# Fused hybrid layer: merge transfers issued by ScalarE, a full-width sine product on VectorE, and score blocks in another order

## What is computed

```python
qa, ka, va, ... = split(rmsnorm(x) @ w_in)          # 12 query heads, 4 key/value heads of 128
qa = apply_rope(rmsnorm(qa), cos, sin) * 128**-0.5  # rope: [t1*cos - t2*sin, t2*cos + t1*sin]
ka = apply_rope(rmsnorm(ka), cos, sin)
# three query groups with (window, dilation) = (128,1), (512,4), (2048,16):
#   causal dilated softmax attention over blocks of 128 queries, previous + own block of keys
o, lse = dilated_group(q[:, :, g], k, v, window, dilation)   # for g in 0, 1, 2
w = softmax(stack(lses)); oa = sum(w * outs)                 # the "merge" of the three groups
```

## Time and profile before

| what | value |
|---|---|
| median of three runs | 1892.96 us |
| profiled execution, its own time | 1892.71 us |
| its span, first to last instruction | 1891.2 us |
| TensorE busy / VectorE / ScalarE / GpSimd | 95% / 58% / 37% / 29% |
| heads 0 to 3 of mixer A (to the transposition of their statistics) | end at 198.5, 333.2, 465.4, 598.2 us |

### The profile page before, as it was taken

One profiled execution on the slowest core, in us unless ns is written; L12 is line 12 of the kernel. 1 busy time (PEld: TensorE's weight loads), 2 busy tenths in 40 slices (PEclk: granted clock), 3 DMA queues, 4 the chain that ended last, 5 costly groups with the idle time before them and its releaser, 6 DMA issues. The chain is left out here.

```text
span 1891.2 us, 27575 instructions
## 1 busy us (share of the span) xinstructions
PE 1797.0 (95%) x9188; PEld 1521.5 (80%) x9188; DVE 1101.1 (58%) x1928; ACT 700.6 (37%) x1598; POOL 551.1 (29%) x654
## 2 busy tenths in 40 slices
PE   6999989999989899999997999999999999999999
PEld 6888877878877888888895888877888888888887
DVE  5362462562652966667576554587555555566786
ACT  5233233233243335353536222453333333334443
POOL 2020230320412705151412000006565555620120
PEclk9999999999999899999999999999999999999999
DMA  7311321421221211111015323214232323178764
GB/s 201 100 35 50 91 95 34 116 74 61 79 78 46 68 46 46 35 33 55 28 72 197 120 83 112 101 67 134 94 105 100 116 89 111 70 251 318 257 213 171
DMA packets 169173, 196.42 MB, mean 104 GB/s; under 512 B 9488, under 2 KB 119344, under 8 KB 168576
## 3 DMA queue, kind: packets, MB, share of 16 engines
q1 hardware_dynamic: 154832, 156.59, 25.9%
q0 software_dynamic: 7984, 28.29, 4.5%
q10 hardware_dynamic: 6272, 10.49, 1.5%
HBM read 150.88 MB, written 44.45 MB: 103 GB/s over the span
## 5 line engine op out<-in xcount | busy, mean ns | idle before, releaser
L2228 PE MATMUL bank<-act_hi,w_hi 128*128 128x512 f32 x568 | 229.1, 403 | 3.9 <-DVE act_lo L1862 3.6
L2230 PE MATMUL bank<-act_hi,w_lo 128*128 128x512 f32 x568 | 222.8, 392 | 0.0
L2229 PE MATMUL bank<-act_lo,w_hi 128*128 128x512 f32 x568 | 222.2, 391 | 0.0
L2228 PE MATMUL bank<-ca,wq 128*128 128x512 f32 x528 | 206.9, 392 | 6.7 <-DVE wq L1973 4.3
L2230 PE MATMUL bank<-ca,wq 128*128 128x512 f32 x528 | 206.0, 390 | 0.0
L2229 PE MATMUL bank<-ca,wq 128*128 128x512 f32 x528 | 205.9, 390 | 0.0
L2228 PE MATMUL bank<-w_hi,act_hi 128*128 128x256 f32 (+1 forms) x576 | 181.3, 315 | 4.0 <-DVE act_lo L1543 3.1
L2229 PE MATMUL bank<-w_lo,act_hi 128*128 128x256 f32 (+1 forms) x576 | 177.7, 308 | 0.0
L2230 PE MATMUL bank<-w_hi,act_lo 128*128 128x256 f32 (+1 forms) x576 | 177.6, 308 | 0.0
L2228 PEld LDWEIGHTS bank<-act_hi,w_hi 128*128 128x128 f32 x568 | 107.6, 189 | 27.6 <-DVE act_lo L1862 4.8
L2230 PEld LDWEIGHTS bank<-act_hi,w_lo 128*128 128x128 f32 x568 | 107.2, 189 | 23.2
(11 more groups left out here) (364 smaller groups left out, 4295.1 us busy)
## 6 DMA issues: line engine op xcount, KB each, us to landing
w_raw<-in_w_in SPq DMA_DIRECT2D x60, 512.0 KB, 4.0
rawd<-in_w_ffn_down SPq DMA_DIRECT2D x99, 256.0 KB, 5.0
rx<-y_scratch SPq DMA_DIRECT2D x77, 256.0 KB, 4.3
wr<-in_w_ffn_gate SPq DMA_DIRECT2D x11, 1024.0 KB, 5.5
wr<-in_w_ffn_up SPq DMA_DIRECT2D x11, 1024.0 KB, 5.4
y_scratch<-sq SPq DMA_DIRECT2D x11, 1024.0 KB, 4.3
y_scratch<-yq SPq DMA_DIRECT2D x33, 256.0 KB, 2.1
gate_scratch<-gbuf ACTq DMA_DIRECT2D x32, 256.0 KB, 2.1
```

What stands on the lines that cost most here:

```text
L2228: pe.matmul(ps, lhs_hi, rhs_hi, start=first, stop=False, skip_group_check=onto)
L2229: pe.matmul(ps, lhs_hi, rhs_lo, start=False, stop=False, skip_group_check=onto)
L2230: return pe.matmul(ps, lhs_lo, rhs_hi, start=False, stop=last, skip_group_check=onto)
```

## The change

Three things are changed, all in mixer A.

1. The merge's transfers are issued by ScalarE and no longer by GpSimd. The store of the statistics stands at the end of `act_head_a`; the eight loads after the squares of s = 0 of the next head; the weights' store at the end of s = 4 and their broadcast load at the end of s = 5. For head 3 they stand at s = 0, 2 and 3 of mixer B's first head.
2. The sine product is one VectorE operation on all 512 columns; GpSimd's half of it is gone (`pool_rope` becomes `pool_rstd`), and so are the waits on `t1_sin`. The subtraction and the addition read the other halves.
3. The order of the batches and their places change. `UNITS` lists the pairs of blocks; the first batch stands at s = 3, two steps stand at s = 8, 11, 13 and 14 (before: 10 to 14). On VectorE `merge_norm` moves from behind `rope(3)` to inside `qk_norm(3)`, and `merge_mul` from s = 5, 8, 8 to s = 6, 7, 8.

```diff
+    def store_stats(eng, h):
+        eng.wait_ge(stat_sbd, h + 1)
+        eng.dma_start(stat_d[bass.ds(h, 1)].rearrange("a u q -> (a u) q"), stat_sb[:, :]).then_inc(stat_out, 16)
+    def load_stats(eng, h):
+        eng.wait_ge(stat_out, 16 * h + 16)
+        eng.wait_ge(c_wgt, 3 * h)
...
+    def store_weights(eng, h):
+        eng.wait_ge(c_wgt, 3 * h + 3)
...
+    def load_weights(eng, h):
+        eng.wait_ge(wgt_out, 16 * h + 16)
+        eng.wait_ge(oa_out, 16 * h)
...
-    UNITS_AT = {6: [0], 7: [1], 8: [2], 9: [3], 10: [4, 5], 11: [6, 7], 12: [8, 9], 13: [10, 11], 14: [12, 13], 15: [14]}
+    UNITS = [(0, 1), (2, 3), (8, 10), (12, 14), (4, 5), (6, 7), (9, 11), (13, 15), (16, 17), (18, 19), (20, 21), (22, 23)]
+    UNITS_AT = {3: [0], 6: [1], 7: [2], 8: [3, 4], 9: [5], 10: [6], 11: [7, 8], 12: [9], 13: [10, 11], 14: [12, 13], 15: [14]}
...
-            pool.wait_ge(t1_gain, 4 * n + 4)
-            pool.wait_ge(rot_done, 2 * n)
-            pool.tensor_tensor(by_tile(rs[:, :, 0:64], j), by_tile(qg[:, :, 64:128], j), table(sin_t, j, 1),
-                               ALU.mult).then_inc(t1_sin, 1)
...
         with pool.Fori(1, H) as h:
-            merge_stats(h - 1)
-            for j in range(4):
-                pool_rope(h, j)
-            merge_weights(h - 1)
-            for j in range(4, 8):
-                pool_rope(h, j)
+            for j in range(8):
+                pool_rstd(h, j)
             merge_sum(h - 1)
         leave_phase(pool)
-        merge_stats(H - 1)
...
-                work = ["d0", "W0", "d1", "d2", "S0", "d3"] + last
+                work = ["d0", "d1", "d2", "S0", "d3"] + last
...
+                if behind and s == 0:
+                    load_stats(act, h - 1)
                 if behind and s == 1:
                     act_weights(h - 1)
+                if behind and s == 4:
+                    store_weights(act, h - 1)
+                if behind and s == 5:
+                    load_weights(act, h - 1)
...
+            store_stats(act, h)
...
-                dve.tensor_tensor(by_tile(rs[:, :, 64:128], j), by_tile(qg[:, :, 0:64], j), table(sin_t, j, 1),
-                                  ALU.mult).then_inc(t1_cos, 1)
+                half = rs[:, :, :].rearrange("p (t m) (a f) -> p t (m a) f", t=2, a=2) if len(QK[j][0]) == 2 else \
+                    rs[:, :, :].rearrange("p m (a f) -> p (m a) f", a=2)
+                dve.tensor_tensor(half, src, table(sin_t, j, 2), ALU.mult).then_inc(t1_cos, 1)
                 dve.wait_ge(t1_cos, 2 * n + 2)
-                dve.wait_ge(t1_sin, n + 1)
...
-                if behind and j == 5:
-                    merge_mul(h - 1, 0)
+                if behind and j == 3:
+                    merge_norm(h - 1)
+                if behind and j in (6, 7):
+                    merge_mul(h - 1, j - 6)
...
-                need = {0: 1, 1: 4, 2: 6, 3: 7, 4: 8}
+                need = {0: 1, 1: 4, 4: 6, 5: 7, 6: 8}
```

More of the change, by code:

```diff
@@ L357, in alone @@
         eng.sem_inc(passed, 1)
+    def store_stats(eng, h):
+        eng.wait_ge(stat_sbd, h + 1)
+        alone(eng)
+        eng.dma_start(stat_d[bass.ds(h, 1)].rearrange("a u q -> (a u) q"), stat_sb[:, :]).then_inc(stat_out, 16)
+    def load_stats(eng, h):
+        sd = stat_d[bass.ds(h, 1)].rearrange("a u q -> (a u) q")
+        eng.wait_ge(stat_out, 16 * h + 16)
+        eng.wait_ge(c_wgt, 3 * h)
+        alone(eng)
+        for q in range(2):
+            r0 = NU * q
+            eng.dma_start(st8[:, q, 0, :], sd[r0:r0 + 8, :]).then_inc(stat_in, 16)
+            for b in range(2):
+                eng.dma_start(st8[4 * b:4 * b + 4, q, 1, :].rearrange("c (r jl) -> c r jl", jl=32),
+                              sd[r0 + 8 + b:r0 + 16:2, :].rearrange("r (jh jl) -> jh r jl", jl=32)
+                              ).then_inc(stat_in, 16)
+            eng.dma_start(st8[:, q, 2, :].rearrange("c (r il) -> c r il", il=16),
+                          sd[r0 + 16:r0 + 24, :].rearrange("r (ih il) -> ih r il", il=16)
+                          ).then_inc(stat_in, 16)
+    def store_weights(eng, h):
+        eng.wait_ge(c_wgt, 3 * h + 3)
+        alone(eng)
+        eng.dma_start(wgt_d[bass.ds(h, 1)].rearrange("a g c t -> c (a g) t"), e8[:, :, :]).then_inc(wgt_out, 16)
+    def load_weights(eng, h):
+        eng.wait_ge(wgt_out, 16 * h + 16)
+        eng.wait_ge(oa_out, 16 * h)
+        alone(eng)
+        eng.dma_start(wb[:, :, :], wgt_d[bass.ds(h, 1)].rearrange("a g c t -> (a g) (c t)").partition_broadcast(P)
+                      ).then_inc(wb_in, 16)
     def leave_phase(eng):
@@ L409, in unit @@
     def unit(b, i):
-        u = 2 * b + i
+        u = UNITS[b][i]
         g, n = u // 8, u % 8
@@ L724, in _, with pool_rstd @@
         enter_phase(pool, 1)
-        def pool_rope(h, j):
+        def pool_rstd(h, j):
             n = 8 * h + j
@@ L1103, in act_head_a @@
                         act.wait_ge(pv_ready, NB * h + (b - 1 if b >= 2 else 0))
-                        if b >= 8:
+                        if not (unit(b, 0)[2] or unit(b, 1)[2]):
                             o, i_ = pt[:, b % 2, :, 1, :], pt_ps.rearrange(
@@ L1208, in act_head @@
                     act_silu(h - 1)
+                if not tail and s == 0:
+                    load_stats(act, H - 1)
                 if not tail and s == 1:
                     act_weights(H - 1)
+                if not tail and s == 2:
+                    store_weights(act, H - 1)
+                if not tail and s == 3:
+                    load_weights(act, H - 1)
         E_AFTER = {2: 0, 3: 1, 5: 2, 6: 3}
@@ L1710, in dve_unit @@
                     dve.wait_ge(masked, NU * h + 2 * j + 2)
-                    dve.tensor_scalar(nmax[:, 2 * j:2 * j + 2], stats[:, 2 * j:2 * j + 2], -SCALE, None,
+                    dve.tensor_scalar(nmax[:, both(j)], stats[:, both(j)], -SCALE, None,
                                       ALU.mult).then_inc(neg_max, 1)
@@ L1716, in dve_unit @@
                     dve.wait_ge(wb_mul, 3 * h)
-                    dve.tensor_copy(u_t[:, 2 * b:2 * b + 2, :],
+                    dve.tensor_copy(u_t[:, both(b), :],
                                     o_ps[:, 2 * P * (b % 2):2 * P * (b % 2) + 2 * P]
@@ L1726, in dve_head_a @@
                     rope(s)
-                    if behind and s == 3:
-                        merge_norm(h - 1)
                 else:
```

51 lines of the change are left out of this document (10 added, 41 removed).

## The result

The changed kernel takes 1904.9 us (median of five runs, 1901.8 to 1905.5); the kernel before, on the same chip, 1893.8 us (five runs). The ratio is 1.0059, 95% interval 1.0044 to 1.0074. The forecast was 1890.5 us with a range to 1901: 14.4 us too low, and on the wrong side. The profiled execution took 1905.5 us with a span of 1903.9 us.

A forecast was written before the change was run, and what follows sets the result against it. TensorE's waits in mixer A (37.5 us, 2% of the time) and the half clock behind them were the bound. 1892.7 - 0.3 (waits) - 1.7 (clock) - 0.6 (mixer B) = 1890.1, given as 1890.5 us; range 1876 to 1901.

The forecast's parts named there:

- Part 1: Transfers moved to ScalarE: stalls at j = 4 and j = 0 go, -11.6 us, nothing given back; 0.35 us an issue.
- Part 2: Sine product as one VectorE operation: 0.69 us, 0.27 us less than before on each j.
- Part 3: Order of blocks: a stall behind s = 8 replaces GpSimd's; waits 37.2 us after, 37.5 before, -0.3 us.
- the three pieces: Behind s = 8, heads 1 to 3: scores wait for `nmax`, transposition for ScalarE, product for `u_done`; 3 us each.
- The other places: Waits: 0.5 us at s = 11, 1.0 at s = 14; those at s = 12 (1.1 to 1.3) go.
- clock term: Half-clock stretches: one in each of heads 1 to 3, perhaps one in head 0; four instead of five, -1.7 us.
- Mixer B: Its first head: the 7.3 us wait changes by -2.5 to +1.8; -0.6 us taken.
- Rival B: Three stops give two half-clock stretches a head, 8 instead of 5: +5 us, 1898; chance 0.16.
- C: Statistics land late, `merge_diffs` on VectorE waits at s = 1: 1894 or 1904; chance 0.1.
- D: The stall does not go: ScalarE's waits for landed transfers block it; time as before, 1893; chance 0.09.
- Rival A: Lag at s = 8 much smaller: 1872 if half of the new waits vanish, 1853 if all; chance 0.2.

The follow-up runs named there:

- e8_sine: The kernel before with only the sine product changed to one VectorE operation: 1886.46 us, ratio 0.9969.
- e6_oldorder: The changed kernel with ScalarE's heads written out and the score blocks in the order of before: 1861.67 us, ratio 0.9842 to the kernel before.
- e11_blocks: The kernel before with only the new order and places of the score blocks: 1915.15 us, ratio 1.0122.
- e13_double8: e10_early_muls with the second step put back behind s = 8, as the change has it: 1867.37 us.
- e10_early_muls: Changed kernel with ScalarE's heads written out, one step behind s = 8, merge products behind the steps of s = 7, 8, 9: 1849.35 us.
- e2_unroll: The changed kernel with ScalarE's heads 1 to 3 written out, no jump back: 1887.16 us, ratio 0.9968 to the kernel before.

## Why the prediction was wrong

The change in steps, each from two kernels: transfers with ScalarE's heads written out and the products at their new places 1892.4 to 1863.9, -28.5; the sine product, and `merge_norm` at its new place, to 1861.7, -2.3; the new order of blocks, to 1887.2, +25.5; ScalarE's loop as it is, to 1904.9, +17.7. Two large gains were given away by two losses, and the forecast had only one of the latter. (Each kernel's median is compared as it stands; the runs of before beside them differ by up to 2 us. The kernel before was not run with its heads written out, so what writing out gives beside the stall, some 3 us by the pairs above, is part of the -28.5 and comes back in the +17.7.)

In the profiled executions mixer A ends 16.0 us later than before (ScalarE's copy of head 3's statistics at 614.94, before 598.98) and the rest of the program is 3.3 us shorter. Against the terms of the forecast:

- **Part 1, "nothing given back", is the step that failed.** Its own points are right: the stall goes, no `rot` wait is left, the issues cost 0.3 to 0.6 us each and lie in gaps, VectorE waits 2.4 us for the statistics in head 1 (forecast about 1.5) and TensorE doesn't see it. But I costed eleven more issues by their durations alone. They come with register work, and ScalarE executes 38 more instructions a head, which moved the branch of its loop from place 555 to 597; ScalarE stands still at each of its two jumps. At its own jump the trace of before showed nothing (0.24 us); but it had the same stall at VectorE's (2.97 and 4.06 us), hidden in the views behind a wait for ScalarE. 11.8 us of `w_lo` waits for 0.9 before: 10.9 us missed.
- **Part 2** is right in size: the product takes 0.69 us and no idle time of VectorE ahead of gains is released by GpSimd for more than 1.3 us. By itself the part gives 6.6 us (`e8_sine`), in the steps above only 2.3 us; that it is mostly covered by then is my reading and not shown.
- **Part 3** is right nearly to the number. Head 0 behind s = 8: 2.2 + 0.8 us of waits, forecast 3.0 + 1.0. Heads 1 to 3 behind s = 8: 2.20 + 2.95 + 4.21 = 9.4 us, forecast 9.0, in the three pieces that it names. The other places: 0.3 and 1.1 us, forecast 0.5 and 1.0. Its rows sum to 36.0 us for 37.2. The bold sentence there ("a stall behind s = 8 has taken its place") is what `e6_oldorder`, `e11_blocks` and `e13_double8` show.
- **The clock term was mis-sized**, with the wrong sign. I had four stretches of 4 us; there are six, at half clock for 3.4 to at least 12 us, two of them behind the jumps. Mixer A's 16.0 us are 9.4 of waits (36.0 + 11.8 for 37.5 + 0.9) and 6.6 of the rest, which I put down to the clock: forecast -1.7, 8.3 us missed. An estimate from the rows of the stretches (TensorE's busy time times the missing share of the clock) gives 14.6 us for these six and 6.6 for the five of before, so the clock is large enough for it. I took a stretch's price from the earlier trace rows (0.57 over 4 us), from a cluster of short waits; behind three waits of 2 to 4 us the clock stood at half for 10 to 12 us and more.
- **Mixer B**: its longest wait is 4.8 us for 7.3, all that my lower bound (-2.5) gave, and with all that follows it is -3.3 us where I took -0.6 (and called it the middle of -2.5 and +1.8, which is -0.35). Executions of one kernel differ by as much (1901.8 to 1905.5 us).

10.9 + 8.3 - 1.2 (waits of part 3) - 2.7 (mixer B and the rest) = 15.3 us, the miss of the profiled execution (1905.5 for 1890.1). That of the medians is 14.4.

Rival B (the clock pays twice) is right in kind: head 0 has a stretch too, and ends 6.0 us later than before with only 1.8 us more of waits. Its 1898 lacks the jump. C and D did not come. Rival A's end of 1853, for a kernel without the new waits, is what `e10_early_muls` (1849) reaches, but not in the kernel as changed.

## What to carry to other kernels

When a change adds instructions to an engine that loops, even ones that lie in gaps, count what it executes per turn and look in the traces of before and after at the first instruction behind each jump, on every engine: idle time put down to "issue" there was a stall of the jump in these kernels, and so was idle time put down to an engine that was already done (VectorE's). It can be written out, or moved away by placing the loop, without touching the work. Where several engines hand a small bank to and fro, put at most one such round behind a stream as long as an engine in it is late, and put work that nobody waits for (the merge products) behind the result that somebody does. Waits of a few us on a busy TensorE cost more than their length once the clock falls behind them, but the factor isn't fixed: 9.4 us of waits went with 18.0 us (`e13_double8` against `e10_early_muls`), 14.1 us with 17.7 (after against `e2_unroll`).

## What was not expected of the hardware

- A jump back cost 0.2 to 0.3 us or 2.6 to 6.9 us, by the place of the loop in the engine's program: with the start at 295 nothing up to a branch at 587 and a stall at 595; with start and branch at 335 and 595 a stall of 6.9 us and a second of 5.0 two instructions on; at 401 and 699 nothing.
- The wait grows with what the DMA engines do beside it: 5.7 us with three loads of 512 KB in flight, 2.6 with them moved away, and the kernel is 10.6 us faster for it.
- 102 semaphore increments in gaps of ScalarE make the changed kernel 14.5 us faster, by moving its loop.
- After waits of 2 to 4 us in a row the granted clock was 0.50 for all of a stretch of 12 us, where a stretch of the kernel before had 3.4 us at half.
